# The first norm of a decoder trunk by pairs of tiles, its shifts on TensorE, and ScalarE's splits moved in the turnovers

## Chip, cores and metric

One core of one Trainium2 chip. The metric is the device time of one execution in microseconds. Engines as in the profile: PE (TensorE; PEld its weight loads), DVE (VectorE), ACT (ScalarE), POOL (GpSimd), SP (SyncE, which issues the transfers).

## What is computed

A trunk of two layers over x (1, 512, 1024), float32 throughout. Layer 0 is FFN, Mamba-2 mixer, FFN; layer 1 is FFN, sliding-window attention over a shared K/V, FFN. Each sub-layer is pre-norm with adaLN:

```python
mod = silu(c) @ mod_w[i] + mod_b[i]          # nine vectors of 1024 per layer
sh1, sc1, g1, shm, scm, gm, sh2, sc2, g2 = split(mod, 9)
h = rmsnorm(x, ffn_norm_w[i, 0]) * (1 + sc1) + sh1
x = x + 0.5 * g1 * ((silu(h @ w_g) * (h @ w_u)) @ w_down)     # D_FF = 2816
...                                          # mixer, second FFN, final norm
```

## The kernel before

**Layout.** x stands transposed: 8 tiles `x[:, j, :]` of 128 features by 512 tokens. Weights come as *slabs* of 128 x 1024 (512 KB, eight 128 x 128 blocks) in the order of use through a ring of four (`RING`). Every product is made of three float32r products (`product3`, L232 to L234): weights and inputs are split into a rounded high part and a low part (the remainder). For a slab ACT makes the high part (`prep_hi`, L222) and DVE the low part (`prep_lo`, L227); SP loads slab n into the ring once `w_lo` says that slab n-4 is split.

**A norm.** For each tile DVE computes x * scale * rstd into `tmp` (L397, here "scaled"), ACT adds the shift and rounds to `h_hi` (L410), and DVE makes the remainder `h_lo` (L390, "rest"), which counts `h_lo_ready` up; PE may use tile j then. `rstd` comes from the squares: PE sums them over partitions with a matrix of ones, and ACT takes Ln and Exp (`rstd_scalar`, L368 and L370), each from another activation table. `log_tables()` (L495) loads Ln's table ahead, `silu_tables()` (L498) silu's.

**Modulation.** A block of 128 outputs of silu(c) @ mod_w is one DVE instruction over 128 x 1024 with a running sum (`mod_block`, L314); its weights are another 512 KB transfer. The blocks 0 to 15 (shift and scale of the first norm, `first_mod`) are loaded and summed before anything else; `mod_collect` (L319) adds the bias. All later blocks are spread over the turns of the first two FFNs.

**Start.** SP issues, in this order: c_row, first_mod 0 and 1, columns, x, first_mod 2 to 10, slabs 0 and 1, first_mod 11 to 15, slabs 2 and 3, then two further mod blocks and the ring. DVE sums all 16, splits slabs 0 and 1, makes `scale_col` and only then runs the norm tile by tile.

**An FFN.** Eleven turns of four slabs (two gate/up pairs u, banks 2u and 2u+1), each pair being 8 tiles k x 2 slabs x 3 products. `leave(u)`: ACT silu, DVE product `tmp[1]` (L637, counts `a_ready`), ACT `a_hi`, DVE `a_lo`. Then the down projection. A *halved* FFN (layer 0's second, layer 1's second) runs turn 0 in two token halves and has no mod blocks in it; in the others turn 0 carries blocks and turn 10 none.

**Turnovers.** Five times (stages st = 1 to 5: before the mixer, second FFN, shared K/V, attention, last FFN) the norm of the next stage is made in two token halves while PE ends the previous one. `turn_over_scalar` places other ACT work between tiles j of half 0:

```python
if j == 0 and late:  prep_hi(act, n1 // 4, 1)
if j == 3:           log_tables()
if j == 4:           square_half(act, st, 1)
if j in (5, 6):      prep_hi(act, n1 // 4, j - 3)
```

`late=True` holds for stages 1, 3 and 4. Behind half 0 DVE makes the low parts of slabs 2 and 3 (`turn_over_vector`), then half 1 begins. PE does half 0 of slabs 0 and 1, half 0 of slabs 2 and 3, then half 1 (in K/V the second is another product of the same size).

Of the kernel before, what the change touches and what calls it, by code (L numbers as in the profile page):

```python
# [21 lines left out]
ALU = mybir.AluOpType  # L22
# [3 lines left out]
P = 128  # L26
# [66 lines left out]

def trunk(nc, w_stream, w_mod, w_dt, x_in, c_in, cols_in, ssm_cols_in, ssm_rows_in, att_rows_in, out):
    ctx = ExitStack()
    with ctx:
# [98 lines left out]
        first_loaded = [sem(f"first_loaded{i}") for i in range(8 * MOD_FIRST)]  # L195
        first_sq_ready = sem("first_sq_ready")
        mod_step, mod_col = sem("mod_step"), sem("mod_col")
        col_step = sem("col_step")
# [215 lines left out]


        def turn_over_scalar(act, st, hs, sh, hi, n1, late=False):
# [147 lines left out]
        def down_mod(mod0):  # L564
            return None if mod0 is None else mod0 + MOD_GU

        def ffn_tensor(pe, k, n0, hs, st, mod0=None, halved=False):
# [1081 lines left out]
        @block.sync  # L1649
        def _(sp):  # L1650
            sp.dma_start(c_row[:, :], c_in.partition_broadcast(P)).then_inc(c_loaded, 16)
            for m in range(8 * MOD_FIRST):
                sp.dma_start(first_mod[:, m, :], w_mod[m]).then_inc(first_loaded[m], 16)  # L1653
                if m == 1:
                    sp.dma_start(cols[:, :], cols_in).then_inc(in_loaded, 16)
                    sp.dma_start(x[:, :, :].rearrange("p j t -> p (j t)"), x_in).then_inc(x_loaded, 16)
                if m == 10:
                    for n in range(2):
                        sp.dma_start(raw[:, n, :], w_stream[n]).then_inc(raw_loaded[n], 16)
            for n in range(2, RING):  # L1660
                sp.dma_start(raw[:, n, :], w_stream[n]).then_inc(raw_loaded[n], 16)
            for m in range(2):
# [81 lines left out]
        def _(pool):  # L1744
# [3 lines left out]
            for n, starts_at_one in enumerate((sq_ready, a_ready, a_lo_ready, y_lo_ready, gstat_done, q_ready, scored, masked,  # L1748
                                               o_done, o_lo_ready)):
                nc.gpsimd.memset(spare[:, n:n + 1], 0.0).then_inc(starts_at_one, 1)  # L1750

            for m, fill in ((after, 0.0), (upto, 1.0), (ident, 0.0)):
                nc.gpsimd.memset(m[:, :], fill).then_inc(ssm_consts, 1)
# [24 lines left out]
        @block.scalar  # L1778
        def _(act):
            act.wait_ge(c_loaded, 16)  # L1780
            nc.scalar.activation(c_row[:, :], c_row[:, :], ACT.Silu).then_inc(c_ready, 1)
            act.wait_ge(x_loaded, 16)
            for j in range(DT):
                nc.scalar.activation(first_sq[:, j, :], x[:, j, :], ACT.Square).then_inc(first_sq_ready, 1)
            act.wait_ge(consts, 1)
            rstd_scalar(act, 0)
            prep_hi(act, 0, 0)
            prep_hi(act, 0, 1)
            act.wait_ge(mod_col, 2)
            norm_scalar(act, 0, M_SH1A, h_hi)  # L1790
            ffn_scalar(act, 0, S_FFN0, 1, mods0, between=lambda: wdt_scalar(act))
            turn_over_scalar(act, 1, 1, M_SHMA, h_hi, S_IN, late=True)
# [15 lines left out]
        def _(dve):  # L1808
            dve.wait_ge(c_ready, 1)
            for v in range(MOD_FIRST):  # L1810
                for k in range(8):
                    mod_block(dve, v, k, first=True)
                if v == 0:
                    dve.wait_ge(in_loaded, 16)
                else:
                    prep_lo(dve, 0, 0)
                    prep_lo(dve, 0, 1)
                mod_collect(dve, v)
            dve.wait_ge(mod_col, 2)
            columns_vector(dve, 1, M_SC1A, col("nw_ffn0"))  # L1820
            norm_vector(dve, 0, 0, M_SH1A, h_hi, h_lo)
            ffn_vector(dve, 0, S_FFN0, M_G1A, 1, mods0, 1, between=lambda: wdt_vector(dve))
            columns_vector(dve, 3, M_SCMA, col("nw_mix0"))
# [44 lines left out]
def lay_out(i):  # L1868
# [30 lines left out]
    for g in range(GROUPS):  # L1899
        order += [z[2 * g], z[2 * g + 1]]  # L1900
        if g < GROUPS - 1:
# [25 lines left out]
    x_t = np.ascontiguousarray(i["x"][0].T.reshape(DT, P, T).transpose(1, 0, 2)).reshape(P, DT * T)  # L1927
    return {"w_stream": stream, "w_mod": w_mod, "w_dt": w_dt, "x_in": x_t, "c_in": np.ascontiguousarray(i["c"][0]),
            "cols_in": np.ascontiguousarray(cols),
# [16 lines left out]
```

## Time and profile before

| | |
|---|---|
| median of 3 runs | 2113.88 us (2113.77 to 2113.98) |
| the profiled execution: time, span | 2114.27 us, 2112.5 us |
| PE, weight loads, DVE, ACT busy | 98%, 81%, 55%, 39% |
| HBM read | 288.36 MB, 138 GB/s over the span |
| mean granted clock of PE | 0.994 |

The busy shares are over the whole span. PE's ends are modelled (a matmul's record overlaps the next), so 98% is not 98% of PE's peak; waits of PE stand beside it in a view of their own.

### The profile page before, as it was taken

What the parts mean: (1) busy time and instruction counts of PE and PEld (TensorE: products, weight loads), DVE (VectorE), ACT (ScalarE), POOL (GpSimd) and SP (SyncE); (2) the same over time, 40 slices, a digit from 0 to 9 for tenths busy, and PEclk for the clock granted to TensorE, in tenths of its full rate; (3) what the DMA queues carried; (4) which work ended last, traced back from release to release, by engine and by line L of the source; (5) the groups of instructions that cost most, each with busy time, mean ns of one, the idle gap of its engine ahead of it and who ended that gap; (6) DMA issues with size and microseconds to landing.
All of it is one profiled execution on the core that took longest, in us unless ns stands there. A gap on an engine that the chain in (4) does not pass through costs nothing.

```text
span 2112.5 us, 27703 instructions
## 1 busy us (share of the span) xinstructions
PE 2063.0 (98%) x10450; PEld 1714.5 (81%) x10450; DVE 1165.1 (55%) x1808; ACT 833.2 (39%) x1296; POOL 4.7 (0%) x29
## 2 busy tenths in 40 slices
PE   4999999999999999999999999999999999999998
PEld 2888888987777778888888888888888788888887
DVE  6555556677777754555566663333337964333333
ACT  4222222467666753422222342223126853222222
POOL 0000000000000000000000000000000000000000
PEclk8999999999999999999999999999999999999999
DMA  7655557435334423455567533332331223322322
GB/s 295 213 187 196 199 188 269 141 108 160 105 111 130 129 70 110 139 186 192 199 216 262 182 100 99 99 98 86 115 109 52 61 60 100 99 92 90 117 90 70
DMA packets 83218, 291.75 MB, mean 138 GB/s; under 512 B 8896, under 2 KB 11712, under 8 KB 83008
## 3 DMA queue, kind: packets, MB, share of 16 engines
q1 hardware_dynamic: 82848, 290.49, 41.8%
q8 instruction: 56, 0.92, 0.2%
q14 instruction: 26, 0.21, 0.0%
q10 hardware_dynamic: 288, 0.13, 0.0%
HBM read 288.36 MB, written 2.23 MB: 138 GB/s over the span
## 4 chain that ended last, share of the span: by engine, by line
PE 89%; DVE 4%; ACT 3%; issue 2%; DMA 1%; SPq 1%; ACTq 0%; DVEq 0%
PE bank L232 28%; PE bank L234 28%; PE bank L233 28%; DVE w_lo_sb L227 1%; DMA first_mod<-w_mod 1%; ACT w_hi_sb L222 1%; PE bank L1346 1%; PE bank L723 1%; PE bank L714 1%; DVE bc L875 1%; PE bank L1361 1%; SPq L1653 1%; PE bank L1381 1%; ACT h_hi L410 1%; DVE tmp L397 1%
## 5 line engine op out<-in xcount | busy, mean ns | idle before, releaser
L232 PE MATMUL bank<-h_hi,w_hi_sb 128*128 128x512 f32 (+1 forms) x1984 | 759.6, 383 | 22.8 <-DVE h_lo L390 18.4
L234 PE MATMUL bank<-h_hi,w_lo_sb 128*128 128x512 f32 (+1 forms) x1984 | 747.2, 377 | 0.0
L233 PE MATMUL bank<-h_lo,w_hi_sb 128*128 128x512 f32 (+1 forms) x1984 | 747.0, 376 | 0.0
L227 DVE TENSOR_TENSOR w_lo_sb<-raw,w_hi_sb 128x1024 fp32r<-128x1024 f32 x356 | 421.4, 1197 | 108.0 <-ACT w_hi_sb L222 102.5
L232 PEld LDWEIGHTS bank<-h_hi,w_hi_sb 128*128 128x128 f32 x1984 | 374.2, 189 | 101.4 <-issue 23.0
L234 PEld LDWEIGHTS bank<-h_hi,w_lo_sb 128*128 128x128 f32 x1984 | 374.0, 188 | 68.6
L233 PEld LDWEIGHTS bank<-h_lo,w_hi_sb 128*128 128x128 f32 x1984 | 374.3, 189 | 66.6 <-issue 1.7
L222 ACT ACTIVATE w_hi_sb<-raw 128x1024 fp32r<-128x1024 f32 x356 | 353.8, 1027 | 70.1 <-PE bank L234 70.0
L637 DVE TENSOR_TENSOR tmp<-tmp,bank 128x512 f32<-128x512 f32 x88 | 60.5, 687 | 418.1 <-ACT tmp L597 216.5
L232 PE MATMUL bank<-a_hi,w_hi_sb 128*128 128x512 f32 (+1 forms) x792 | 290.7, 367 | 0.0
L234 PE MATMUL bank<-a_hi,w_lo_sb 128*128 128x512 f32 (+1 forms) x792 | 290.0, 366 | 0.0
L233 PE MATMUL bank<-a_lo,w_hi_sb 128*128 128x512 f32 (+1 forms) x792 | 289.9, 366 | 0.0
L597 ACT ACTIVATE tmp<-bank 128x512 f32<-128x512 f32 x88 | 52.6, 598 | 558.4 <-PE bank L234 558.4
L314 DVE SCALAR_TENSOR_TENSOR mod_raw<-mod_raw,c_row 128x1024 f32<-128x1024 f32 x144 | 175.7, 1220 | 33.4 <-DMA mod_raw<-w_mod 32.1
L233 PEld LDWEIGHTS bank<-a_lo,w_hi_sb 128*128 128x128 f32 x792 | 149.5, 189 | 24.4
L232 PEld LDWEIGHTS bank<-a_hi,w_hi_sb 128*128 128x128 f32 x792 | 149.5, 189 | 24.0
L234 PEld LDWEIGHTS bank<-a_hi,w_lo_sb 128*128 128x128 f32 x792 | 149.5, 189 | 24.0
L331 ACT ACTIVATE tmp<-x_trunk 128x512 f32<-128x512 f32 x35 | 22.2, 633 | 299.2 <-DVE x_trunk L535 260.9
L640 DVE TENSOR_TENSOR a_lo<-tmp,a_hi 128x512 f32 (+1 forms) x88 | 61.0, 693 | 80.8 <-ACT a_hi L599 80.8
L535 DVE SCALAR_TENSOR_TENSOR x_trunk<-bank,gate_col,x_trunk 128x512 f32<-128x512 f32 x28 | 21.0, 750 | 128.0 <-PE bank L234 128.0
L599 ACT ACTIVATE a_hi<-tmp 128x512 f32 (+1 forms) x88 | 55.6, 632 | 91.1 <-DVE tmp L637 91.1
L397 DVE SCALAR_TENSOR_TENSOR tmp<-x_trunk,scale_col,rstd 128x256 f32<-128x256 f32 (+1 forms) x96 | 49.6, 527 | 17.3 <-issue 16.2
(207 smaller groups left out, 1613.8 us busy)
## 6 DMA issues: line engine op xcount, KB each, us to landing
raw<-w_stream SPq DMA_DIRECT2D x356, 512.0 KB, 4.1
mod_raw<-w_mod SPq DMA_DIRECT2D x144, 512.0 KB, 4.6
first_mod<-w_mod SPq DMA_DIRECT2D x16, 512.0 KB, 14.5
sums<-sums_rows SPq DMA_DIRECT2D x7, 1024.0 KB, 8.9
decays<-decay_rows SPq DMA_DIRECT2D x8, 768.0 KB, 4.2
x_trunk<-x_in SPq DMA_DIRECT2D x1, 2048.0 KB, 10.5
trunk_out<-x_trunk SPq DMA_DIRECT2D x2, 512.0 KB, 2.8
trunk_out<-x_trunk SPq DMA_DIRECT2D x4, 256.0 KB, 2.1
```

What stands on the lines that cost most here:

```text
L222: nc.scalar.activation(w_hi_sb[:, s, 0:width], raw[:, s, 0:width], ACT.Copy).then_inc(w_hi, 1)
L227: nc.vector.tensor_tensor(w_lo_sb[:, s, 0:width], raw[:, s, 0:width], w_hi_sb[:, s, 0:width], ALU.subtract).then_inc(w_lo, 1)
L232: nc.tensor.matmul(ps, s_hi, m_hi, start=start, stop=False)
L233: nc.tensor.matmul(ps, s_hi, m_lo, start=False, stop=False)
L234: return nc.tensor.matmul(ps, s_lo, m_hi, start=False, stop=stop)
L314: nc.vector.scalar_tensor_tensor(w, w, 1.0, c_row[:, :], ALU.mult, ALU.mult, accum_out=to).then_inc(mod_step, 1)
L331: nc.scalar.activation(tmp[:, 0, :], x[:, j, :], ACT.Square).then_inc(sq_ready, 1)
L397: nc.vector.scalar_tensor_tensor(norm_tile(j, hf), x[:, j, at], scale_col[:, j:j + 1], rstd[:, at], ALU.mult, ALU.mult).then_inc(t_ready, 1)
L597: nc.scalar.activation(tmp[:, 0, :], bank[2 * u][:, :], ACT.Silu).then_inc(silu_done, 1)
L599: nc.scalar.activation(a_hi[:, f, :], tmp[:, 1, :], ACT.Copy).then_inc(a_hi_ready, 1)
L637: nc.vector.tensor_tensor(tmp[:, 1, :], tmp[:, 0, :], bank[2 * u + 1][:, :], ALU.mult).then_inc(a_ready, 1)
L640: nc.vector.tensor_tensor(a_lo[:, f, :], tmp[:, 1, :], a_hi[:, f, :], ALU.subtract).then_inc(a_lo_ready, 1)
```

## The change

1. **Order of the start.** x is loaded first, in two halves, and squared by halves. The scale of the first norm stays on DVE, but by pairs of tiles: sums for two tiles, bias, `scale_col`, two "scaled", two "rest". The shift blocks of tiles 0 and 1 too stay on DVE; the shifts of tiles 2 to 7 are computed on PE from a re-laid copy `w_first` (three parts of 1 MB): eight float32 matmuls with silu(c) in 32 equal columns (`c_32`) give rows on four groups of 32 partitions (`shift_rows`), ACT copies them to SBUF (`copy_rows`), and two matmuls with a column that has a one at partitions 0, 32, 64 and 96 sum the groups and turn them into columns (`shift_columns`).
2. **Turn 0 on PE** becomes `first_quad`: all four slabs, tile by tile in a written order, with these steps between them. `keep_warm` issues float32 matmuls of ones whose result is not used.
3. **Slabs' low parts** 0 to 3 stand behind or between remainders in `first_norm_vector`.
4. **The first FFN is halved**: no mod blocks in turn 0, and `slabs_and_mods` loads them a turn later.
5. **Turnovers**: `log_tables` and the two `prep_hi` move as below.

```diff
+        def first_norm_vector(dve):
...
+            for v in (M_SC1A, M_SH1A):
+                sum_of(v, 0)
+                sum_of(v, 1)
+            collect(0)
+            dve.wait_ge(rs_step, 2)
+            for b in range(DT // 2):
+                if b:
+                    sum_of(M_SC1A, 2 * b)
+                    sum_of(M_SC1A, 2 * b + 1)
+                    collect(b)
+                scaled(2 * b)
+                scaled(2 * b + 1)
+                if b == 0:
+                    prep_lo(dve, 0, 0)
+                rest(2 * b)
+                if b == 0:
+                    prep_lo(dve, 0, 1)
+                rest(2 * b + 1)
+                if b == 1:
+                    prep_lo(dve, 0, 2)
+                    prep_lo(dve, 0, 3)
...
         def turn_over_scalar(act, st, hs, sh, hi, n1, late=False):
             def between(j):
                 if j == 0 and late:
                     prep_hi(act, n1 // 4, 1)
+                if j == 2 and late:
+                    prep_hi(act, n1 // 4, 2)
...
-                if j == 3:
-                    log_tables()
                 if j == 4:
                     square_half(act, st, 1)
-                if j in (5, 6):
-                    prep_hi(act, n1 // 4, j - 3)
+                if j == DT - 1:
+                    if not late:
+                        prep_hi(act, n1 // 4, 2)
+                    prep_hi(act, n1 // 4, 3)
+                    log_tables()
...
+        def first_quad(pe):
+            def pair_step(u, k):
+                pe.wait_ge(h_lo_ready, k + 1)
+                w = slice(k * P, (k + 1) * P)
+                for l in range(2 * u, 2 * u + 2):
+                    if k == 0:
+                        pe.wait_ge(w_lo, l + 1)
+                    mm = product3(bank[l][:, :], w_hi_sb[:, l, w], w_lo_sb[:, l, w], h_hi[:, k, :], h_lo[:, k, :],
+                                  k == 0, k == 7)
+                    if k == 7:
+                        mm.then_inc(slab_used, 1)
...
+            def shift_rows(b):
+                pe.wait_ge(first_loaded[2 * b], 16)
...
+                for k in range(DT):
+                    g = slice(32 * (k % 4), 32 * (k % 4) + 32)
+                    mm = nc.tensor.matmul(bank[4 + b % 2][g, 0:2 * P], c_32[:, k, :], w[:, k * 2 * P:(k + 1) * 2 * P],
+                                          start=k < 4, stop=k >= 4)
+                mm.then_inc(rows_made, 1)
+
+            def shift_columns(b):
+                pe.wait_ge(rows_copied, b)
+                for t in range(2):
+                    mm = nc.tensor.matmul(bank[6 + b % 2][:, t:t + 1], shift_row[:, b % 2, t * P:(t + 1) * P],
+                                          spare[:, 16:17], start=True, stop=True)
+                mm.then_inc(shift_turned, 1)
+
+            shift_rows(1)
+            pair_step(0, 0)
+            shift_columns(1)
+            pair_step(0, 1)
+            keep_warm(pe, 12, 4)
+            pair_step(0, 2)
+            shift_rows(2)
+            pair_step(0, 3)
+            shift_columns(2)
+            pair_step(1, 0)
+            pair_step(1, 1)
+            shift_rows(3)
+            pair_step(1, 2)
+            shift_columns(3)
+            for k in range(4, 8):
+                pair_step(0, k)
+                pair_step(1, k - 1)
+            pair_step(1, 7)
...
+                if first and k == 0:
+                    first_quad(pe)
+                    pe.wait_ge(a_ready, ONE + 1)
+                    return
...
+            sp.dma_start(c_32[:, :, :].rearrange("p k m -> p (k m)"), c_32_in).then_inc(c_32_loaded, 16)
+            for part, loaded in enumerate((x_loaded, x_rest_loaded)):
...
             sp.dma_start(c_row[:, :], c_in.partition_broadcast(P)).then_inc(c_loaded, 16)
...
+            load_first(DT)
+            load_first(DT + 1)
+            sp.dma_start(cols[:, :], cols_in).then_inc(in_loaded, 16)
+            load_first(0)
+            load_first(1)
+            first_slab(0)
+            first_slab(1)
+            for b in range(1, DT // 2):
+                first_shifts(b)
+                load_first(DT + 2 * b)
+                load_first(DT + 2 * b + 1)
+                if b == 1:
+                    first_slab(2)
+                    first_slab(3)
...
-            slabs_and_mods(6, 8 * mods0 + 2, False)
+            slabs_and_mods(6, 8 * mods0 + 2, True)
...
+            def between(j):
+                if j == 1:
+                    prep_hi(act, 0, 1)
+                if j in (1, 3, 5):
+                    copy_rows(j // 2 + 1)
+                if j == 1:
+                    prep_hi(act, 0, 2)
+                    prep_hi(act, 0, 3)
+            norm_scalar(act, 0, M_SH1A, h_hi, None, between)
...
             pe.wait_ge(slab_used, RING)
+            keep_warm(pe, 20)
...
             mm.then_inc(stat_done, 1)
-            ffn_tensor(pe, 0, S_FFN0, 0, 1, mods0)
+            pe.wait_ge(rs_step, 2)
+            keep_warm(pe, 16)
+            pe.wait_ge(quarter_row, 5)
+            ffn_tensor(pe, 0, S_FFN0, 0, 1, mods0, halved=True)
```

In ACT's part silu of `c_32` comes first, then the squares by halves of x, silu of c_row, `log_tables`, rstd and `prep_hi` of slab 0.

## Rows read from the trace of the kernel before

**Rows 1.** Busy time of each engine, from the page (us, share, instructions)

```profile
PE 2063.0 (98%) x10450; PEld 1714.5 (81%) x10450; DVE 1165.1 (55%) x1808; ACT 833.2 (39%) x1296; POOL 4.7 (0%) x29
```

**Rows 2.** The chain that ended last, shares by engine

```profile
PE 89%; DVE 4%; ACT 3%; issue 2%; DMA 1%; SPq 1%; ACTq 0%; DVEq 0%
```

**Rows 3.** Waits of PE over the span: total us, times, longest

```profile
PE bank L232 <- DVE h_lo L390: 18.4, 6, 15.6
...
PE bank L232 <- DVE w_lo_sb L227: 4.8, 9, 1.3
```

**Rows 4.** Timeline of the start: start, us, engine, line, operation, operands, [idle before, releaser]

```profile
5.27 1.06 ACT L1781 ACTIVATE c_row<-c_row 128x1024 f32<-128x1024 f32 x1 [3.17 <-DMA c_row<-c_in]
...
13.99 9.88 PE L1855 MATMUL bank<-first_sq,ones 128*128 128x512 f32 x16 [13.99 <-ACT first_sq L1784]
...
27.80 1.99 ACT L222 ACTIVATE w_hi_sb<-raw 128x1024 fp32r<-128x1024 f32 x2
...
28.19 1.23 DVE L314 SCALAR_TENSOR_TENSOR first_mod<-first_mod,c_row 128x1024 f32<-128x1024 f32 x1 [2.53 <-DMA first_mod<-w_mod]
...
36.81 0.17 DVE L374 SCALAR_TENSOR_TENSOR scale_col<-mod,cols 128x8 f32<-128x8 f32 x1
37.01 1.42 DVE L397 SCALAR_TENSOR_TENSOR tmp<-x_trunk,scale_col,rstd 128x512 f32<-128x512 f32 x2
...
39.52 0.79 PE L232 MATMUL bank<-h_hi,w_hi_sb 128*128 128x512 f32 x1 [15.64 <-DVE h_lo L390]
...
64.78 0.69 DVE L637 TENSOR_TENSOR tmp<-tmp,bank 128x512 f32<-128x512 f32 x1 [1.67 <-PE bank L234]
```

**Rows 5.** Stretches of the start: length, PE busy, granted clock, DMA share, GB/s

```profile
20.00:30.00 10.00, 3.88 (x10) 0.82 1.03 420
30.00:40.00 10.00, 0.48 (x1) 0.50 1.02 401
40.00:50.00 10.00, 10.00 (x38) 0.83 0.10 33
```

**Rows 6.** Timeline of the turnover at stage 2: ACT, DVE, PE's weight loads

```profile
841.81 1.28 ACT L495 ACT_TABLE_LOAD   x1
843.10 0.51 ACT L410 ACTIVATE h_hi<-tmp,mod 128x256 fp32r<-128x256 f32 x1
...
847.04 0.48 DVE L390 SCALAR_TENSOR_TENSOR h_lo<-tmp,mod,h_hi 128x256 fp32r<-128x256 f32 x1 [0.86 <-ACT h_hi L410]
847.44 2.35 DVE L227 TENSOR_TENSOR w_lo_sb<-raw,w_hi_sb 128x1024 fp32r<-128x1024 f32 x2
...
844.18 0.19 PEld L232 LDWEIGHTS bank<-h_hi,w_hi_sb 128*128 128x128 f32 x1 [0.92 <-DVE h_lo L390]
...
849.85 0.19 PEld L232 LDWEIGHTS bank<-h_hi,w_hi_sb 128*128 128x128 f32 x1 [0.72 <-DVE w_lo_sb L227]
```

**Rows 7.** Timeline of PE's weight loads, turnovers at stages 3 and 5

```profile
1214.97 0.19 PEld L232 LDWEIGHTS bank<-w_hi_sb,hkv_hi 128*128 128x128 f32 x1 [1.49 <-DVE w_lo_sb L227]
...
1740.33 0.19 PEld L232 LDWEIGHTS bank<-h_hi,w_hi_sb 128*128 128x128 f32 x1 [1.24 <-DVE h_lo L390]
```

**Rows 8.** The chain in order of time at the scan: start, us, what

```profile
531.72 0.23 PE bank L232
...
532.40 0.59 PE bank L714 x8
532.99 0.63 PE bank L723 x2
533.62 0.22 PE bank L702 x2
...
540.02 0.22 PE bank L718 x4
```

**Rows 9.** Timeline of PE's weight loads just before the clock rose

```profile
42.67 0.33 PEld L234 LDWEIGHTS bank<-h_hi,w_lo_sb 128*128 128x128 f32 x1
43.09 0.33 PEld L232 LDWEIGHTS bank<-h_hi,w_hi_sb 128*128 128x128 f32 x1
```

More of the change, by code:

```diff
@@ L413, in norm_scalar, with sum_of, collect, scaled @@
                     between(j)
+        def first_norm_vector(dve):
+            made = [0]
+            def sum_of(v, j):
+                mod_block(dve, v, j, first=True)
+                made[0] += 1
+            def collect(g):
+                two = slice(2 * g, 2 * g + 2)
+                b = cols[:, COLS["modb"][0]:COLS["modb"][1]].rearrange("p (v j) -> p v j", j=DT)
+                w = COLS["nw_ffn0"][0]
+                if g:
+                    dve.wait_ge(shift_turned, g)
+                else:
+                    dve.wait_ge(in_loaded, 16)
+                dve.wait_ge(mod_step, made[0])
+                for v in (M_SH1A, M_SC1A):
+                    made_in = bank[6 + g % 2][:, 0:2] if g and v == M_SH1A else mod[:, v, two]
+                    op = nc.vector.tensor_tensor(mod[:, v, two], made_in, b[:, v, two], ALU.add)
+                    if v == M_SC1A and g:
+                        made[0] += 2
+                        op.then_inc(mod_step, 2)
+                        dve.wait_ge(mod_step, made[0])
+                    elif v == M_SC1A:
+                        op.then_inc(first_step, 1)
+                        dve.wait_ge(first_step, 1)
+                    elif 2 * g + 2 == DT:
+                        op.then_inc(mod_col, MOD_FIRST)
+                op = nc.vector.scalar_tensor_tensor(scale_col[:, two], mod[:, M_SC1A, two], 1.0,
+                                                    cols[:, w + 2 * g:w + 2 * g + 2], ALU.add, ALU.mult)
+                if 2 * g + 2 == DT:
+                    op.then_inc(col_step, 1)
+                    dve.wait_ge(col_step, 1)
+                else:
+                    op.then_inc(first_step, 1)
+                    dve.wait_ge(first_step, g + 2)
+            def scaled(j):
+                if j > 1:
+                    dve.wait_ge(h_lo_ready, j - 1)
+                nc.vector.scalar_tensor_tensor(norm_tile(j, None), x[:, j, :], scale_col[:, j:j + 1], rstd[:, :],
+                                               ALU.mult, ALU.mult).then_inc(t_ready, 1)
+            def rest(j):
+                dve.wait_ge(h_hi_ready, j + 1)
+                nc.vector.scalar_tensor_tensor(h_lo[:, j, :], norm_tile(j, None), mod[:, M_SH1A, j:j + 1], h_hi[:, j, :],
+                                               ALU.add, ALU.subtract).then_inc(h_lo_ready, 1)
+            for v in (M_SC1A, M_SH1A):
[19 more added lines that the diff above has]
+                    prep_lo(dve, 0, 3)
@@ L565, in down_mod, with keep_warm @@
             return None if mod0 is None else mod0 + MOD_GU
+        def keep_warm(pe, count, b=7):
+            for _ in range(count):
+                nc.tensor.matmul(bank[b][:, 0:P], ones[:, :], ones[:, :], start=True, stop=True)
+        def first_quad(pe):
[12 more added lines that the diff above has]
+                if b == 1:
+                    pe.wait_ge(c_32_ready, 1)
+                if b == 3:
+                    pe.wait_ge(rows_copied, 1)
+                w = first_mod[:, 2 * b:2 * b + 2, :].rearrange("p j d -> p (j d)")
+                for k in range(DT):
[27 more added lines that the diff above has]
+            pair_step(1, 7)
         def ffn_tensor(pe, k, n0, hs, st, mod0=None, halved=False):
@@ L1750, in _ @@
                 nc.gpsimd.memset(spare[:, n:n + 1], 0.0).then_inc(starts_at_one, 1)
+            nc.gpsimd.memset(spare[:, 16:17], 0.0).then_inc(quarter_row, 1)
+            pool.wait_ge(quarter_row, 1)
+            for g in range(4):
+                nc.gpsimd.memset(spare[32 * g:32 * g + 1, 16:17], 1.0).then_inc(quarter_row, 1)
+                pool.wait_ge(quarter_row, g + 2)
             for m, fill in ((after, 0.0), (upto, 1.0), (ident, 0.0)):
@@ L1779, in _ @@
         def _(act):
+            act.wait_ge(c_32_loaded, 16)
+            nc.scalar.activation(c_32[:, :, :], c_32[:, :, :], ACT.Silu).then_inc(c_32_ready, 1)
+            for j in range(DT):
+                act.wait_ge(x_loaded if j < 4 else x_rest_loaded, 16)
+                nc.scalar.activation(first_sq[:, j, :], x[:, j, :], ACT.Square).then_inc(first_sq_ready, 1)
             act.wait_ge(c_loaded, 16)
             nc.scalar.activation(c_row[:, :], c_row[:, :], ACT.Silu).then_inc(c_ready, 1)
-            act.wait_ge(x_loaded, 16)
-            for j in range(DT):
-                nc.scalar.activation(first_sq[:, j, :], x[:, j, :], ACT.Square).then_inc(first_sq_ready, 1)
+            log_tables()
             act.wait_ge(consts, 1)
@@ L1787, in _, with copy_rows @@
             prep_hi(act, 0, 0)
[L1788 to L1791, printed above, removed]
+            def copy_rows(b):
+                act.wait_ge(rows_made, b)
+                if b == 3:
+                    act.wait_ge(shift_turned, 1)
+                nc.scalar.activation(shift_row[:, b % 2, :], bank[4 + b % 2][:, 0:2 * P], ACT.Copy).then_inc(rows_copied, 1)
+            def between(j):
[7 more added lines that the diff above has]
+            norm_scalar(act, 0, M_SH1A, h_hi, None, between)
+            ffn_scalar(act, 0, S_FFN0, 1, mods0, halved=True, between=lambda: wdt_scalar(act))
             turn_over_scalar(act, 1, 1, M_SHMA, h_hi, S_IN, late=True)
@@ L1809, in _ @@
             dve.wait_ge(c_ready, 1)
[L1810 to L1822, printed above, removed]
+            first_norm_vector(dve)
+            ffn_vector(dve, 0, S_FFN0, M_G1A, 1, mods0, 1, halved=True, between=lambda: wdt_vector(dve))
             columns_vector(dve, 3, M_SCMA, col("nw_mix0"))
```

33 lines of the change are left out of this document (21 added, 12 removed).

## Prediction, written before the changed kernel was run

> **What bounds the kernel now.** I read the engine summary first: PE is busy 98% of the span [rows 1], and the chain that ended last lies on PE for 89% of it [rows 2]. So nothing that only frees DVE or ACT can pay; what can pay is time in which PE stands idle or runs slowly. Then the waits of PE over the whole span: by far the largest is one wait of 15.6 us for `h_lo`, which stands in front of the first product; the other waits for `h_lo` make 2.8 us and those for `w_lo_sb` 4.8 us [rows 3]. Then the start-up as a timeline. The reader is to see that PE's own sums of squares occupy it from 13.99 to 23.87, that the first product starts at 39.52, and that DVE can read the second pair of banks of turn 0 (its end) only at 64.78 [rows 4]. Before the first product DVE sums sixteen blocks of modulation weights at 1.23 us, and waits for transfers, the last time 2.53 us [rows 4], while the DMA engines are fully busy at 401 to 420 GB/s [rows 5]. The start is therefore bound by the load of 16 x 0.52 MB in front of any product, with DVE right behind it. In the stretch 30 to 40 PE's granted clock is 0.50 (1.2 GHz) after it had done nothing since 23.87, and it is up again (0.83 on average) in 40 to 50 [rows 5]. Last, the turnovers between stages: PE waits there for a remainder behind a table load, and for the low parts of slabs [rows 6, 7].
>
> **The start, part by part.** Prices: one sum over 1024 elements 1.23 us [rows 4]; `scaled` 0.71 us, from two in 1.42 [rows 4], and `rest`, the same operation on the same shape, as much; one `prep_hi` 1.0 and one `prep_lo` 1.15, both from pairs [rows 4, 6]; a small column operation 0.2, from 36.81 to the next start at 37.01 [rows 4]; a full-width split matmul 0.227 us at 2.4 GHz, written 0.23 in the chain [rows 8], and 0.42 at 1.2 GHz, from 42.67 to 43.09 [rows 9]. So a `pair_step` (2 slabs x 3 products) is 1.36 or 2.55 us, and the 16 of turn 0 are 21.8 us at the full clock. Before, turn 0 took 64.6 - 39.5 = 25.1 us: 21.8, 1.8 for nine slow ones, and a stall of 1.3 for a slab's low part [rows 3].
>
> Transfers. Before block 12 lay 10.6 MB (c_row, 13 blocks, x, cols, 2 slabs), and it was there at 28.19 at 0.42 MB/us, so a byte position M lands at about 3.0 + M/0.42. In the new order M is 1.2 for x's first half, 2.2 for its second, 2.75 for c_row, 3.8 for the first two scale blocks, 5.0 with the first two shift blocks, 6.0 with slabs 0 and 1, 7.1 with the first `w_first` part, then 8.1 (scale 2, 3), 9.2 (slabs 2, 3), 10.2, 11.3, 12.3, 13.4 (scale 6, 7). In us: 6, 8, 9.5, 12, 15, 17, 20, 22, 25, 27, 30, 32, 35. The bytes are the same as before; the last block lands some 3 us later, because slabs 2 and 3 stand ahead of it.
>
> ACT and DVE. ACT squares x by half-tiles from 6 to 10.5, then silu of c_row (1.06 us, [rows 4]) to 11.7. PE's sums of squares cost 9.88 us before, of which the first part was at the low clock; behind 20 warming matmuls I take 8 x 0.85 = 6.8 us (four times the 0.22 of one float32 product of 128 columns, in two records [rows 8], less its rounding), 8.3 to 15.1, and rstd to 17.8 (two ACTIVATEs and one table load). DVE: four sums 11.7 to 16.7, `collect(0)` 0.6, then two `scaled` 17.9 to 19.3, prep_lo 0, rest 0 at 21.2, prep_lo 1, rest 1 at 23.2. Each later pair costs two sums 2.5, collect 0.6, two `scaled` and two `rest` 2.9: 6.0 us, and pair 1 has two prep_lo (2.4) behind it. So `h_lo` is there at 21.2, 23.2, 28.5, 29.2, 36.9, 37.6, 42.9, 43.7; the last two were waited for from 35 on, so DVE, not the transfer, sets them, with 2.6 us to spare. DVE has six sums fewer than before (7.4 us), because six shift blocks go to PE.
>
> The new work on PE. `shift_rows` is 8 float32 matmuls of 256 columns on four groups of 32 output columns. No row shows four groups. Lower bound: two groups of 64 do run together, for four records on two groups take 0.22 us, where the two records of one 128-column product cost 0.22 alone; a change of grouping costs 0.15 to 0.2, as 0.59 for 8 records and 0.63 for a plain 256-column one (0.43 by its columns) show [rows 8]. Four groups at once give 2 x 0.43 + 0.35 = 1.2 us. Upper bound, all in series: 8 x 0.43 = 3.4, twice that at the low clock. I take 1.2, since the pairs in the rows do run side by side. The Trainium skill (TensorEngine Tiling (Array Packing), Key Properties) says that tiles operate independently and that a change of mode drains the engine; by that rule the block costs 1.2 too, and the trace agrees as far as two groups go.
>
> PE's order then: 16 warmers from 17.8 to 21.3, rows 1 to 22.4, (0,0) once slab 1's low part is there, to 23.8, columns, (0,1) to 25.4, 12 warmers to 28.0, (0,2) 28.5 to 29.9, rows 2, (0,3) to 32.4, columns, (1,0) and (1,1) to 35.3, rows 3, (1,2), columns to 38.0. From there PE never waits: nine steps of 1.36 end at 50.3. Each `shift_turned` comes before DVE asks (24.0 for 25.7, 32.6 for 34.1, 38.0 for 40.1), so it costs nothing; late by its upper bound it would hold DVE's next `scaled`. Warmers fill only time in which PE has no input. Then the halved turn makes PE wait for `a_ready`: from the release of slab 0 (46.9) ACT does two prep_hi and a silu (2.6 us), DVE the second low part and the product, to 51.0. That is a stall of 0.7 us that before did not exist. Behind it slabs 6 and 7 have 11 us for some 8 us of DVE work, hidden.
>
> Start of turn 1: 64.6 before, 51.0 after, **-13.6 us**. Bounds: at best DVE-paced with nothing on top, -15; with serial shift blocks PE ends at 56.6, DVE is held up to 4 us, and it is -7. Moving blocks of layer 0 one turn later (halved) keeps their number, and no PE wait stands in the second layer, which is queued that way: 0.
>
> **The turnovers.** Five of them. The ACT_TABLE_LOAD of 1.28 us leaves the place after tile 3 of half 0, where PE then waited 0.92 us for `h_lo` [rows 6]. The two prep_hi (1.05 each) leave the places between tiles 5, 6 and 7, where rest 7 had to wait until 847.04; without both, DVE's two-instruction period of 0.8 us brings it to 845.3. In the plain turnovers (stages 2 and 5) both prep_hi then follow tile 7, and slab 2's low part is bound by ACT (846.3 + 1.2), the next one at 848.7, against 847.44 + 2.35 = 849.8 [rows 6]: -1.1. PE waited 0.72 for exactly that part [rows 6]. Stage 5 has a further wait of 1.24 for `h_lo` [rows 7]; the same count gives -1.4. In the late ones (1, 3, 4) one prep_hi goes into a gap that ACT has while DVE does a low part, so ACT never delays the pair of low parts, and it is earlier by the whole 1.7: PE gains 1.65, 1.7 (the K/V stage waits 1.49 for it [rows 7]) and 1.65 (each with a wait of 0.72 like that of [rows 6]). Sum **-7.5 us**. Price of the move: the table load and prep_hi now stand before the second half's rstd, which is 1.1 us later in the plain ones and 0.1 to 0.2 in the late ones. It is covered: the first `h_lo` of half 1 would be there at 852.5, and PE asks at 848.7 + 5.4 = 854.1 (15 groups of three half-width products, 0.12 each by half of 0.23); tile 8 has 1.2 us left. Without the cover it would cost up to 1.1 each. Lower bound of the gain: only the 0.7 of each `w_lo_sb` wait, 3.5 in all; upper 8.5, all waits for remainders too.
>
> The Trainium skill (ScalarE: Activation LUTs, What ACT_TABLE_LOAD costs) puts a switch at 2.66 us with its drain. The trace differs: the load at 841.81 is 1.28 and the next tile starts at 843.10. By the page the moved load would bring half 1 within 0.2 us of PE's request, and the plain turnovers would win about 1 us each still, so the sum would be -7.3.
>
> **Sum.** The profiled execution's span is 2112.5 and its time 2114.27. 2112.5 - 13.6 - 7.5 = 2091.4; with the 1.8 around it 2093.2, and as that execution lies 0.4 above the median of the runs, **2092.8**.
>
> **Rivals.** (A) The shift blocks run in series or late, PE becomes the bound of the start: start -7, sum -14.5, 2099.4. For: four groups are in no row. Against: two groups side by side. (B) Only the start or only the turnovers pay. Turnovers nil (half 1 is late after all): 2100.3. Start nil, as if the first `h_lo` could not move, because transfers land out of the order of issue and pair 0 waits behind 13 MB: 2106.4. Against: before, c_row, issued first, was there by 5.27 with everything else behind it [rows 4]. (C) Slower: PE runs the whole of turn 0 at 1.2 GHz, because its input comes in drops and the warmers do not hold the clock. Place: 17.8 to the end of (1,7). Warmers 6.8, three shift blocks 2.1 each, DVE held 4 us by the first columns, 16 steps at 2.55: end at 78, 13.5 later than before, less 7.5: 2119.9. Of the 27 us between this and the forecast 21 must be lost before it is slower, so about three quarters of that work must be slow. For: the clock did fall in the idle stretch [rows 5]. Against: it rose within the first nine matmuls' work once they came back to back, and from 31 on my schedule has no gap. (D) The change does what it says but the gain is returned later: a stage bound by a transfer waits as before. Up to half returned, 2103. Against: PE's waits in rows 3 are few, and none is for a DMA.
>
> **Chances.** Forecast (2089 to 2097) 0.58; A 0.15; B 0.12; D 0.06; C 0.05; a mixture that ends within 0.2% 0.04. 0.2% (4.2 us) is about what can be told from no change. Faster 0.90, same 0.05, slower 0.05. The range reaches from the best bounds of both parts (-15 and -8.5, 2090, and a little for what I price too high) over A, both B and D: 2087 to 2106.
>
> **What would show it.** First product near 22.4 rather than 39.5; steps of 0.23 us spacing and clock 1.0 from about 20 on; `shift_rows` at 1.2 us; DVE's last `h_lo` of the first norm near 43.7; the product of turn 0's first pair read near 50, turn 1 begun near 51; no table load between tiles 3 and 4 of a turnover; slab 3's low part 1.1 to 1.7 us sooner after the stage's end, and no PE wait for `h_lo` in half 1. The forecast is wrong if blocks land much later than the table of positions says, if PE waits for `shift_turned` or `a_ready` for more than 2 us, or if the clock is 0.5 beyond 28 us.

## The result, and the profile after

| | before | changed |
|---|---|---|
| median | 2113.86 us (6 runs) | 2097.11 us (6 runs) |
| ratio | | 0.9918, 95% interval 0.9907 to 0.993 |
| the profiled execution: time, span | 2114.27, 2112.5 | 2097.26, 2095.5 |

The kernel is 16.8 us (0.8%) faster, where 21.1 was forecast. One execution of the changed kernel, of 4214.17 us, is disturbed: it counts among the six of the median, but is left out of the ratio (the other five have a median of 2096.95).

The engine summary and the chain, then PE's waits over the span, which answer to [rows 1], [rows 2] and [rows 3] (L238 to L240 are now the three products, L396 and L467 the remainders, L780 the product of an FFN turn):

```profile
PE 2075.7 (99%) x10606; PEld 1727.2 (82%) x10606; DVE 1158.0 (55%) x1805; ACT 836.9 (40%) x1300; POOL 5.1 (0%) x34
...
PE 90%; DVE 5%; ACT 3%; issue 2%; DMA 0%; ACTq 0%; DVEq 0%; SPq 0%; POOL 0%; POOLq 0%
```

```profile
PE bank L650 <- ACT rstd L376: 2.8, 1, 2.8
PE bank L238 <- DVE w_lo_sb L233: 1.2, 3, 0.5
...
PE bank L238 <- DVE h_lo L396: 1.0, 4, 0.5
PE bank L238 <- DVE tmp L780: 1.0, 1, 1.0
...
PE bank L857 <- DVE el L1285: 0.5, 2, 0.3
```

The 15.6 us wait for the first remainder is gone, and those for low parts fell from 4.8 to 1.2 us. One wait is new: 1.0 us for the product of turn 0, at the start of turn 1. The last row, two waits of 0.3 us in the mixer's scan, is used below.

The timeline of the start, which answers to [rows 4] (L650 the warmers, L2030 the sums of squares, L676 a shift block, L462 the tiles before the shift):

```profile
1.07 6.11 PE L650 MATMUL bank<-ones 128*128 128x128 f32 x40 [1.07 <-POOL ones L1907]
7.14 7.13 PE L2030 MATMUL bank<-first_sq,ones 128*128 128x512 f32 x16
17.06 5.47 PE L650 MATMUL bank<-ones 128*128 128x128 f32 x32 [2.79 <-ACT rstd L376]
22.46 1.07 PE L676 MATMUL bank<-first_mod,c 128*32 128x256 f32 x16
23.46 0.50 PE L238 MATMUL bank<-h_hi,w_hi_sb 128*128 128x512 f32 x1
...
29.51 0.50 PE L238 MATMUL bank<-h_hi,w_hi_sb 128*128 128x512 f32 x1
...
27.00 1.06 ACT L228 ACTIVATE w_hi_sb<-raw 128x1024 fp32r<-128x1024 f32 x1 [1.11 <-DMA raw<-w_stream]
27.96 1.32 ACT L416 ACTIVATE h_hi<-tmp,mod 128x512 fp32r<-128x512 f32 x2
...
28.70 1.41 DVE L467 SCALAR_TENSOR_TENSOR h_lo<-tmp,mod,h_hi 128x512 fp32r<-128x512 f32 x2 [1.33 <-ACT h_hi L416]
...
42.64 1.42 DVE L467 SCALAR_TENSOR_TENSOR h_lo<-tmp,mod,h_hi 128x512 fp32r<-128x512 f32 x2
...
53.30 0.49 PE L238 MATMUL bank<-h_hi,w_hi_sb 128*128 128x512 f32 x1 [1.04 <-DVE tmp L780]
```

The reader is to see the first product at 23.46 in place of 39.52, the 16 warmers (the float32 matmuls of `keep_warm`) that took 5.47 us (32 records) and not the 3.5 of the forecast, tile 2's remainder waiting 1.33 us for ACT, which had just waited for a slab's landing, and turn 1 at 53.30. Stretches of the start, which answer to [rows 5] (length, PE busy, granted clock, DMA share, GB/s):

```profile
16.00:18.00 2.00, 0.94 (x6) 0.91 1.02 420
18.00:20.00 2.00, 2.00 (x11) 0.50 1.04 440
20.00:22.00 2.00, 2.00 (x15) 0.74 0.97 399
22.00:24.00 2.00, 2.00 (x23) 1.00 1.04 424
```

The clock fell to 1.2 GHz after the 2.79 us idle behind the sums of squares, so the warmers ran for more than half of their 5.47 us at it; it was up (1.00) when the products came.

The turnover at stage 2, which answers to [rows 6]:

```profile
832.72 2.00 ACT L228 ACTIVATE w_hi_sb<-raw 128x1024 fp32r<-128x1024 f32 x2
834.73 1.28 ACT L575 ACT_TABLE_LOAD   x1
...
832.85 0.48 DVE L396 SCALAR_TENSOR_TENSOR h_lo<-tmp,mod,h_hi 128x256 fp32r<-128x256 f32 x1 [0.18 <-ACT h_hi L416]
833.79 2.36 DVE L233 TENSOR_TENSOR w_lo_sb<-raw,w_hi_sb 128x1024 fp32r<-128x1024 f32 x2 [0.46 <-ACT w_hi_sb L228]
838.26 0.88 DVE L403 SCALAR_TENSOR_TENSOR tmp<-x_trunk,scale_col,rstd 128x256 f32<-128x256 f32 x2 [2.11 <-ACT rstd L376]
...
831.13 0.19 PEld L238 LDWEIGHTS bank<-h_hi,w_hi_sb 128*128 128x128 f32 x1 [0.41 <-DVE h_lo L396]
836.21 0.19 PEld L238 LDWEIGHTS bank<-h_hi,w_hi_sb 128*128 128x128 f32 x1 [0.72 <-DVE w_lo_sb L233]
```

PE still waits 0.72 us for slab 3's low part, but sooner; and DVE now waits 2.11 us for the second half's rstd, which is the price of the moved table load and is covered: no wait of PE for a remainder stands behind it.

How much each stage gave: PE's first statistics matmul of each turnover stands at the same place in both programs, so the difference of its times is what was won up to there. Two such rows of before, then the same two of the changed kernel:

```profile
396.37 0.41 PEld L361 LDWEIGHTS bank<-tmp,ones 128*128 128x128 f32 x2
835.37 0.41 PEld L361 LDWEIGHTS bank<-tmp,ones 128*128 128x128 f32 x2
```

```profile
385.34 0.41 PEld L367 LDWEIGHTS bank<-tmp,ones 128*128 128x128 f32 x2
822.83 0.41 PEld L367 LDWEIGHTS bank<-tmp,ones 128*128 128x128 f32 x2
```

| up to the statistics of stage | before | changed | won up to here | won since the last | forecast |
|---|---|---|---|---|---|
| 1 | 396.37 | 385.34 | 11.03 | 11.03 (start) | 13.6 |
| 2 | 835.37 | 822.83 | 12.54 | 1.51 | 1.65 |
| 3 | 1198.78 | 1185.13 | 13.65 | 1.11 | 1.1 |
| 4 | 1586.03 | 1571.43 | 14.60 | 0.95 | 1.7 |
| 5 | 1730.82 | 1715.19 | 15.63 | 1.03 | 1.65 |
| 6 (the end) | 2094.94 | 2077.89 | 17.05 | 1.42 | 1.4 |

### The profile page after: what moved, and what is told of

Read it like the earlier page. It is cut to its first block, busy times and chain, and to the rows that moved or that the text cites. A ratio compares the mean times of both kernels' runs of the same rounds, so it can differ in the third digit from the quotient of the medians.

```text
span 2095.5 us, 28023 instructions
## 1 busy us (share of the span) xinstructions
PE 2075.7 (99%) x10606; PEld 1727.2 (82%) x10606; DVE 1158.0 (55%) x1805; ACT 836.9 (40%) x1300; POOL 5.1 (0%) x34
## 4 chain that ended last, share of the span: by engine, by line
PE 90%; DVE 5%; ACT 3%; issue 2%; DMA 0%; ACTq 0%; DVEq 0%; SPq 0%; POOL 0%; POOLq 0%
PE bank L238 28%; PE bank L239 28%; PE bank L240 28%; DVE tmp L403 1%; DVE w_lo_sb L233 1%; PE bank L1489 1%; PE bank L650 1%; PE bank L866 1%; PE bank L857 1%; DVE bc L1018 1%; PE bank L1504 1%; DVE h_lo L396 1%; PE bank L1524 1%; ACT w_hi_sb L228 1%; DMA sums<-sums_rows 0%
## 5 line engine op out<-in xcount | busy, mean ns | idle before, releaser
L238 PE MATMUL bank<-h_hi,w_hi_sb 128*128 128x512 f32 (+1 forms) x1984 | 757.6, 382 | 4.3 <-DVE h_lo L396 1.0
L240 PE MATMUL bank<-h_hi,w_lo_sb 128*128 128x512 f32 (+1 forms) x1984 | 745.3, 376 | 0.0
L238 PEld LDWEIGHTS bank<-h_hi,w_hi_sb 128*128 128x128 f32 x1984 | 373.4, 188 | 82.1 <-issue 6.9
L240 PEld LDWEIGHTS bank<-h_hi,w_lo_sb 128*128 128x128 f32 x1984 | 373.3, 188 | 68.3
L238 PE MATMUL bank<-a_hi,w_hi_sb 128*128 128x512 f32 (+1 forms) x792 | 290.1, 366 | 0.0
L240 PE MATMUL bank<-a_hi,w_lo_sb 128*128 128x512 f32 (+1 forms) x792 | 289.4, 365 | 0.0
L780 DVE TENSOR_TENSOR tmp<-tmp,bank 128x512 f32<-128x512 f32 x88 | 60.5, 688 | 412.3 <-ACT tmp L740 207.6
L238 PEld LDWEIGHTS bank<-a_hi,w_hi_sb 128*128 128x128 f32 x792 | 149.4, 189 | 24.4
L240 PEld LDWEIGHTS bank<-a_hi,w_lo_sb 128*128 128x128 f32 x792 | 149.4, 189 | 24.0
L403 DVE SCALAR_TENSOR_TENSOR tmp<-x_trunk,scale_col,rstd 128x256 f32<-128x256 f32 (+1 forms) x88 | 43.7, 507 | 26.4 <-issue 16.2
```

The costliest lines, as they stand in the source:

```text
L238: nc.tensor.matmul(ps, s_hi, m_hi, start=start, stop=False)
L240: return nc.tensor.matmul(ps, s_lo, m_hi, start=False, stop=stop)
L403: nc.vector.scalar_tensor_tensor(norm_tile(j, hf), x[:, j, at], scale_col[:, j:j + 1], rstd[:, at], ALU.mult, ALU.mult).then_inc(t_ready, 1)
L780: nc.vector.tensor_tensor(tmp[:, 1, :], tmp[:, 0, :], bank[2 * u + 1][:, :], ALU.mult).then_inc(a_ready, 1)
```

## Experiments

All medians below stand beside runs of the kernel before on the same chip: 2114.1 for the first four, 2114.05 for the second four, 2113.99 and 2113.88 for the last two pairs. Twelve runs were made. Where a run is compared with the changed kernel, its median is taken from 2096.93 (the repeat below); the result's 2097.11 would make each gain 0.2 larger.

**The two halves apart.** The first has the new start with ACT's old turnover order, the second the old start with the new order:

```diff
-                if j == 2 and late:
-                    prep_hi(act, n1 // 4, 2)
+                if j == 3:
+                    log_tables()
...
-                if j == DT - 1:
-                    if not late:
-                        prep_hi(act, n1 // 4, 2)
-                    prep_hi(act, n1 // 4, 3)
-                    log_tables()
+                if j in (5, 6):
+                    prep_hi(act, n1 // 4, j - 3)
```

> The changed kernel with ScalarE's turnover order as it was before (Ln's table after tile 3, the two high-part splits after tiles 5 and 6). Theory: the two halves of the change add up, and in the traces the start gave 11.0 us up to the first turnover: 2113.9 - 11.0 = 2102.9 us. Rival: part of what the traces show at the turnovers is owed to the new start (slabs and modulation loads queued elsewhere), then this run lies nearer the changed kernel's 2097, under 2101.

> The kernel before with only ScalarE's new turnover order. Theory: 1.5, 1.1, 0.95, 1.0 and 1.4 us at the five turnovers, 6.0 in all: 2107.9 us. Rival: they need the new start, or the moved table load makes the second half late when the start is the old one: 2111 to 2114 us.

2103.32 us (ratio 0.9948, 0.9931 to 0.9964) and 2107.61 (0.997, 0.9958 to 0.9981): 10.8 and 6.5 us, together 17.3, against 16.8 for both (17.1 by the repeat). The halves add up, and neither needs the other. In the second run's trace stage 1 gave 2.2 us and the others 1.1, 0.94, 1.0 and 1.42, close to the table. The ten other traces with both halves give 1.7 to 2.2 for stage 1, so its 1.51 in the table is the low end of a scatter. The scatter lies in the mixer's scan, where PE waits for `el` (a product that DVE makes there) 0.3 us at a time: twice in the changed kernel's trace, once in two of the ten others (the 1.7 and a 1.9), and in none of the eight that gave 2.0 to 2.2. The kernel before has one such wait:

```profile
PE bank L714 <- DVE el L1142: 0.3, 1, 0.3
```

The run with only the new start has none, and gave 0.3 us in this stage with the turnovers as they were. So of the 2.0 us some 1.7 are the turnover's, against 1.65 forecast.

**No warmers.**

> The changed kernel without its three groups of warming matmuls (20, 16 and 12); nothing that the output needs is left out. Theory: without them the clock is at 1.2 GHz from the sums of squares on and while tiles 0 to 3 arrive; the tensor engine is what ends turn 0 from 29.5 us on, and it would do the first 4 us from there at half speed: 2 to 3 us longer than the changed kernel, 2099 to 2100. Rival: the warmers do nothing but fill time, or even delay (the 16 stood in front of the first shift block): 2096 to 2097.3.

2097.26 us (0.992, 0.9903 to 0.9936): no change, and the theory fell. The clock was at 1.2 GHz from 19 to about 26, and the first shift block and step (0,0) ran at half speed:

```profile
18.00:20.00 2.00, 0.00 (x0) 0.77 1.02 434
20.00:22.00 2.00, 0.66 (x8) 0.50 0.98 401
22.00:24.00 2.00, 2.00 (x14) 0.50 1.03 420
24.00:26.00 2.00, 2.00 (x8) 0.52 1.05 436
26.00:28.00 2.00, 1.94 (x11) 1.00 1.00 420
28.00:30.00 2.00, 0.07 (x1) 1.00 1.00 412
```

But behind that slow work it rose again, so step (0,1), from 26.30, ran at full speed, and in the 2.00 us that PE then stood idle before (0,2) it stayed up:

```profile
23.20 0.80 PE L238 MATMUL bank<-h_hi,w_hi_sb 128*128 128x512 f32 x1
...
26.30 0.48 PE L238 MATMUL bank<-h_hi,w_hi_sb 128*128 128x512 f32 x1
...
29.93 0.50 PE L238 MATMUL bank<-h_hi,w_hi_sb 128*128 128x512 f32 x1 [2.00 <-DVE h_lo L467]
```

(0,2) came at 29.93, where the changed kernel's two traces have 29.51 and 29.80, and turn 1 at 53.74, where they have 53.30 and 53.55.

**Shift blocks in series.**

```diff
-                    g = slice(32 * (k % 4), 32 * (k % 4) + 32)
+                    g = slice(0, 32)
...
```

> The changed kernel with all eight matmuls of a shift block on one group of 32 output columns, so that they can't run side by side; the columns are made from these 32 partitions. Theory: a block takes 8 x 0.43 = 3.4 us in place of 1.1, and the second and third lie in the stretch in which the tensor engine never waits, so turn 0 ends 4.7 us later: 2101.7 (more if VectorE is held up by the columns). Rival: VectorE's pairs set the end of turn 0, not the tensor engine, and the blocks have room: 2097 to 2098.

2104.39 us (0.9954, 0.9938 to 0.9971), 7.5 us longer. The twelve warmers and (0,2), then the second block, with its columns behind the step that follows; below them DVE's remainders of tiles 2 and 3:

```profile
29.09 2.84 PE L650 MATMUL bank<-ones 128*128 128x128 f32 x24
31.68 0.48 PE L238 MATMUL bank<-h_hi,w_hi_sb 128*128 128x512 f32 x1
...
33.25 3.64 PE L676 MATMUL bank<-first_mod,c 128*32 128x256 f32 x16
38.41 0.60 PE L683 MATMUL bank<-spare,shift_row 32*128 32x1 f32 x4
...
29.68 1.42 DVE L467 SCALAR_TENSOR_TENSOR h_lo<-tmp,mod,h_hi 128x512 fp32r<-128x512 f32 x2
```

A block takes 3.64 us against 1.07. From the warmers at 18.12 to the end of turn 0 PE has no wait in this trace, so all three blocks count in full, 7.7 us and not the 5.1 of two: the first too, because the twelve warmers stand behind it in PE's order and keep (0,2) until 31.68, though its remainder was there by 30.4. Each column step also took 0.17 us longer, and the first block began 0.57 earlier; that makes 7.65, and turn 1 begins 7.8 later (61.12 for 53.30). DVE is held up in each `collect` (2.17, 3.39 and 2.98 us for the columns), but PE waits for none of it, so this costs nothing here.

**The four places where the forecast was missed.** Each edit is made to the changed kernel alone.

```diff
-            for k in range(4, 8):
-                pair_step(0, k)
-                pair_step(1, k - 1)
-            pair_step(1, 7)
+            pair_step(0, 4)
+            pair_step(0, 5)
+            pair_step(1, 3)
+            pair_step(0, 6)
+            pair_step(0, 7)
+            for k in range(4, 8):
+                pair_step(1, k)
```

> The changed kernel with the last nine steps of turn 0 in another order: (0,4), (0,5), (1,3), (0,6), (0,7), then (1,4) to (1,7). Theory: slabs 0 and 1 are released 2.7 us earlier, so the two low parts and the product on which the tensor engine waits for 1.04 us at the start of turn 1 are done in time: 1.0 to 1.2 us less than the changed kernel, about 2095.9. Rival: the wait is not set by the release of slab 0 but by what ScalarE and VectorE do after the norm, or (0,6) now comes before its remainder: no change, 2097.

2095.17 us (0.9911, 0.9894 to 0.9927). The wait at the start of turn 1 is gone from the trace, and the first statistics stand at 383.98, 1.36 before those of the changed kernel (385.34).

```diff
                 if j == 1:
                     prep_hi(act, 0, 1)
+                if j == 3:
+                    prep_hi(act, 0, 2)
+                    prep_hi(act, 0, 3)
                 if j in (1, 3, 5):
                     copy_rows(j // 2 + 1)
-                if j == 1:
-                    prep_hi(act, 0, 2)
-                    prep_hi(act, 0, 3)
...
-            keep_warm(pe, 16)
+            keep_warm(pe, 8)
...
-            keep_warm(pe, 12, 4)
```

> The changed kernel with ScalarE's high parts of slabs 2 and 3 behind tile 3 of the first norm in place of behind tile 1, and warmers cut to 20, 8 and 0 (the 12 would now stand in front of step (0,2)). Theory: tile 2 waited on ScalarE, in order, behind the landing of slab 3 at 27.0 us; now its remainder is there 1.0 to 1.4 us earlier and turn 0 ends as much earlier: 2095.6 to 2096.1. Rival: the second part of the shift weights or slab 3's low part is what comes last there, or the clock falls without warmers: 2097 or more.

2095.74 us (0.9913, 0.9896 to 0.9929), 1.2 us less by the medians. Step (0,2) began at 28.87 against 29.51, and the first statistics stand 0.63 earlier; so about half of the 1.2 is this edit, and the rest lies within the scatter of stage 1. The edit moves the splits and takes out warmers at once; this run does not separate the two.

```diff
-            pool.wait_ge(slab_used, RING + S_Q)
+            pool.wait_ge(slab_used, RING + S_Q + 1)
```

> The changed kernel with GpSimd's masks for the attention made one slab later (after the first query slab), out of the fourth turnover's first half. Theory: two VectorE operations of 0.48 us took 0.74 and 0.84 beside these, which in the new order is on the path to slab 3's low part: 0.6 us less, 2096.4 (the fourth turnover then gives 1.6 as the first does). Rival: that turnover is short for another reason, no change: 2097.

2096.29 us (0.9916, 0.9899 to 0.9933). The same two DVE operations in the changed kernel, then in this one:

```profile
1580.49 0.74 DVE L403 SCALAR_TENSOR_TENSOR tmp<-x_trunk,scale_col,rstd 128x256 f32<-128x256 f32 x1
1581.15 0.84 DVE L396 SCALAR_TENSOR_TENSOR h_lo<-tmp,mod,h_hi 128x256 fp32r<-128x256 f32 x1
```

```profile
1580.40 0.48 DVE L403 SCALAR_TENSOR_TENSOR tmp<-x_trunk,scale_col,rstd 128x256 f32<-128x256 f32 x1
1580.79 0.48 DVE L396 SCALAR_TENSOR_TENSOR h_lo<-tmp,mod,h_hi 128x256 fp32r<-128x256 f32 x1
```

From stage 4's statistics to stage 5's it is now 143.15 us (1571.33 to 1714.48) against 143.76: the 0.61 that was missing.

```diff
-                if j == 4:
+                if j == 3:
                     for l in range(2):
                         act.wait_ge(slab_used, RING + S_KV + l + 1)
```

> The changed kernel with ScalarE's two copies of the keys behind tile 3 of the following norm in place of tile 4. Theory: the third turnover's gain is 1.7 us, but 0.7 of it is given back at the end of the K/V stage, where the tensor engine waits 0.65 us for the keys' copy; now it waits 0 to 0.3: 2096.5. Rival: it is the fifth slab's low part (its end lies 0.5 us before the wait's end), which this doesn't move: 2097.

2096.05 us (0.9915, 0.9898 to 0.9931). PE's waits between 1190 and 1230 in the changed kernel:

```profile
PE bank L238 <- DVE w_lo_sb L233: 0.5, 1, 0.5
PE bank L238 <- ACT k_all L1432: 0.5, 1, 0.5
```

Here the second is gone, and stage 3's statistics to stage 4's take 385.58 us (1184.55 to 1570.13) against 386.30, 0.72 less.

**All four together**, and the changed kernel once more on the same chip:

> The changed kernel with the four edits of the last group together (pair 0 first, splits behind tile 3 with fewer warmers, GpSimd's masks later, the keys' copy earlier). Theory: their causes are apart, so the gains add up: 1.5 + 1.2 + 0.7 + 0.9 = 4.3 us below the changed kernel, about 2092.7. Rival: the first two share a limit (VectorE's last two remainders, from which (0,6) and (0,7) start), and only the larger of them counts: 2093.9 or more.

> The changed kernel once more, for a comparison on the same chip with the run of all four edits: 2096 to 2097.3 us, the spread being that of the clock's fall at about 18 us and of its rise.

2093.69 us (0.9905, 0.9889 to 0.992) against 2096.93 (0.9919, 0.9906 to 0.9933): 3.2 us, not 4.3. The traces account for it: 1.95 us up to the first statistics (385.55 to 383.60), 0.8 and 0.6 at the two later places, less some 0.4 between the statistics of stages 2 and 3, whose cause is not shown. The traces of the single edits had sized them at 1.36, 0.63, 0.72 and 0.61, 3.3 in all, so they add up; the 4.3 had been taken from medians, in which stage 1's scatter (0.4 to 0.6 us of each single edit's gain by its trace) is counted with every edit. The two edits of the start do not share a limit of DVE, for (0,6) and (0,7) start without a wait. But (0,2) began only at 29.07; in this trace the clock had fallen before the 8 warmers, and it was still at 1.2 GHz in the first shift block and step (0,0).

**The warmers again**, once with the four edits, once in the changed kernel:

> The four edits together, but with the 16 warmers behind rstd kept at 16 and only the 12 left out. Theory: with 8 the clock was at 1.2 GHz in the first shift block and in steps (0,0) and (0,1), so the first columns came 0.5 us late for VectorE and (0,2) began at 29.07; with 16 it begins at 28.2 to 28.6 and all ends 0.5 to 0.9 us earlier: 2092.8 to 2093.2. Rival: VectorE's sums or the landing of slab 2 set that step, no change: 2093.7.

> The changed kernel without the 12 warmers in front of step (0,2), ScalarE's order unchanged. Theory: ScalarE's order (tile 2 behind the landing of slab 3) sets that step at 29.4 to 29.5, the warmers only end as late: 2096.9, no change. Rival: the warmers themselves delay it: 2096.3 or less; or the clock falls and it is 2098 or more.

The first gave 2092.95 us (0.9901, 0.9884 to 0.9917), 4.0 below the changed kernel, with (0,2) at 28.26: as expected, and the fastest version made. That it lies on the forecast's 2092.8 is chance, for the forecast had none of these edits. In its trace the clock had not fallen before the warmers (1.00 from 16 to 22, where the trace with 8 has 0.69 and 0.50 from 18 to 22), so the two traces differ in more than the edit; the medians differ by 0.7 us, and no run of the one overlaps a run of the other. The second gave 2098.26 (0.9925, 0.9908 to 0.9941). Three of its four runs (2098.26, 2098.26, 2099.18) lie above those of the changed kernel (2095.95 to 2097.27), the fourth (2096.72) does not: the theory was wrong that nothing hangs on the 12, though not every execution pays. PE's timeline and the granted clock of that run:

```profile
25.61 0.40 PE L240 MATMUL bank<-h_hi,w_lo_sb 128*128 128x512 f32 x1
29.59 0.67 PE L238 MATMUL bank<-h_hi,w_hi_sb 128*128 128x512 f32 x1 [3.59 <-DVE h_lo L467]
30.06 0.63 PE L239 MATMUL bank<-h_lo,w_hi_sb 128*128 128x512 f32 x1
```

```profile
28.00:30.00 2.00, 0.41 (x1) 0.94 1.02 420
30.00:32.00 2.00, 2.00 (x6) 0.50 1.07 451
32.00:34.00 2.00, 2.00 (x18) 0.70 0.96 397
```

The step is no earlier (29.59), so the warmers did not delay it, and it waits for the remainder, which stands behind ACT; but PE had idled 3.59 us, the clock fell just there, and the stretch that PE never makes up began at half speed.

## Why the prediction came out as it did

**Direction, place and mechanism** were right, and the two parts were the right two. The start, read as bound by 16 blocks ahead of any product, gave 10.8 us when run alone, and the turnovers 6.5. The size was too high: 2097.1 lies at the upper edge of the forecast's 2089 to 2097. What is not separated is the start itself: no run takes the pairs of tiles without the shifts on PE, or either without the new order of loads and the halved FFN, so what each of these is worth is argued from the schedule and not shown.

**The start's term, -13.6, measured -11.2** (64.48 to 53.30 for turn 1). Three terms of the schedule were mis-sized, 2.3 us together. (1) `h_lo` of tile 2 was put at 28.5 and PE's step (0,2) there; it was 29.5. I had slab 3 landing at 25, and it landed at 27.0. Two splits stand in front of tile 2 in ACT's order, the last of them slab 3's, and the schedule had no term for that. At 25 it would have needed none; at 27.0 tile 2's rounding began at 27.96. By the profile's stretches 9.5 MB had been moved by 26, more than the 9.2 that stand up to slab 3 in the order of issue, so part of the 2 us is later transfers that went beside it (an estimate from these two numbers). (2) From (0,2) to the end of turn 0 I had 21.8 us of work, and it took 22.6. The 14 steps took 19.7 us and not 19.0, the excess being mostly in the first step behind a shift block or a pause (1.5 for 1.36), and the two column steps 0.36 each where I had left 0.2; the two blocks took 1.1 each, not 1.2. (3) The stall for `a_ready` was put at 0.7 us and the gap was 1.2; reordering the last steps removed it, which shows it.

**The four column groups** do run at once: 1.07 us for a block against my 1.2, and 3.64 in series. The Trainium skill (TensorEngine Tiling (Array Packing), Key Properties) says that tiles run independently, and by these two numbers the trace agrees. Rival A was real as a mechanism, 7.5 us long, but not what the change does. I had bounded it at 6.6 for the start, with DVE held up to 4 us as part of it; the run has PE itself, in order, as the bound.

**DVE's pace** was right within 0.4 us at the end: the last remainders of the first norm were made from 42.64 to 44.06, where 43.7 was forecast for the end, and each `shift_turned` but the first came in time (that one 0.17 us late).

**The clock.** I took the 16 warmers at the high clock, 3.5 us; in the profile of the result it had fallen, and they took 5.47, hidden behind DVE but for the 0.17 us by which the first columns were late. In the repeat's trace the clock did not fall, after the same 2.79 us, and they took 3.84. Rival C is refuted for this order: even with no warmers at all the low clock lasted only until about 26. Its own time was also added up too high: the terms named (6.8, three times 2.1, 4 and 16 times 2.55 behind 17.8) end at 75.7 and not at 78, which gives 2117.6. What the warmers buy depends on which stretch they close: none at all was as good as all, and leaving out only the last 12 cost 1.3 us by the medians.

**The turnovers, -7.5, measured -6.0 to -6.5.** Stages 2 and 5 came out at 1.11 and 1.42 for 1.1 and 1.4, and stage 1 at some 1.7 for 1.65 once the waits in the scan are set apart. Stage 3's low part was earlier by 1.66 us as forecast (1214.97 - 1198.78 before, 1199.66 - 1185.13 after), but 0.7 was given back where I had not looked: ACT's copies of the keys, which come behind the now unhurried second half. This is rival D in small, and moving the copies gave it back. Stage 4 missed 0.6, since GpSimd's masks fall into the same window; before, the same two operations took 0.74 and 0.60 us beside the same masks, hidden behind the table load (1594.15 to 1595.43) that the change moved away. My cover for half 1 held: DVE waits 2.11 us for rstd in stage 2, and PE has no `h_lo` wait behind it. On the table load, the Trainium skill's 2.66 us with drain (ScalarE: Activation LUTs, What ACT_TABLE_LOAD costs) again is not what the trace has: from 834.73 to the next ACTIVATE at 836.02 are 1.29 us.

**Rival B** (one half pays nothing) is refuted by the two runs with one half each.

## To carry to other kernels

Where an engine works in order, follow a late transfer through that engine's queue to everything behind it, not only to the tile that needs it: slab 3's landing, two splits ahead of one tile, cost the start about 1 us, the largest of the three terms that were off. When a stall is removed, look at what it had been hiding; here it was GpSimd's work beside DVE's in one stage and the copies of the keys in another. Warm-up matmuls are worth what the idle stretch in front of bound work costs, so judge each group by the granted clock of the stretch behind it. One trace is not enough for that: two executions of the same program differed in whether the clock fell.

## What the runs showed of the hardware

- Eight float32 matmuls of 32 output columns and 256 moving columns took 1.07 us on four column groups and 3.64 us on one.
- Two VectorE operations of 0.48 us took 0.74 and 0.84 us while GpSimd made masks, and 0.48 when it did not.
- After 2.79 us without matmuls behind the sums of squares the clock fell in the profile of the changed kernel, and in that of its repeat, the same program, it stayed (16 warmers took 5.47 and 3.84 us).
- Before (0,2) it stayed up over 2.00 us without matmuls in the run without warmers, and fell after 3.59 us in the run without the last 12. The second is 1.0 us longer than the first by the medians, and its runs spread over 2.5 us (2096.72 to 2099.18), where those of the changed kernel spread over 1.3.
